# Three inner norms of a two-layer encoder, with the tokens run in two halves

## What is computed

```python
for layer in range(2):
    h = rms_norm(x, norm_mix_pre[layer])
    m = even_mixer(h, ...) if layer == 0 else odd_mixer(h, ...)   # both end in @ w_out, 1024 x 1024
    x = x + rms_norm(m, norm_mix_post[layer])
    h = rms_norm(x, norm_ffn_pre[layer])
    u = causal_dwconv(h @ w_up, conv_w, conv_b)      # w_up 1024 x 5632, three taps
    g, val = u[..., :2816], u[..., 2816:]
    f = (gelu(g) * val) @ w_down                     # 2816 x 1024
    x = x + rms_norm(f, norm_ffn_post[layer])
```

## Time and profile before

| what | value |
|---|---|
| three runs | 1189.26, 1192.99, 1192.96 us; median 1192.96 |
| the profiled execution | 1188.73 us; its span 1186.9 us |
| TensorE busy | 1149.5 us, 97% of the span |
| VectorE, ScalarE, GpSimd busy | 58%, 41%, 6% |
| mean granted TensorE clock | 0.993 of full speed |
| HBM read | 98.02 MB |
| load of a 1 MB unit | 5.1 us from issue to landing (median) |
| what ends the chain: TensorE, VectorE, ScalarE | 84%, 7%, 6% of the span |

### The profile page before, as it was taken

The page is one execution under the profiler, slowest core; times in us unless marked ns, Lnnn a source line. Parts: engine busy times, 40 slices in busy tenths (PEclk is TensorE's granted clock), DMA queues, the critical chain, the costliest instruction groups (busy, mean ns, idle before and its releaser), DMA issues.

```text
span 1186.9 us, 14989 instructions
## 1 busy us (share of the span) xinstructions
PE 1149.5 (97%) x5888; PEld 959.4 (81%) x5888; DVE 692.9 (58%) x840; ACT 486.1 (41%) x667; POOL 73.2 (6%) x57
## 2 busy tenths in 40 slices
PE   8999999999999999999999998899999999999997
PEld 6875777777888888888887788786888888899997
DVE  5745455558876766732228677248877766752222
ACT  4555655434533443431123229334444443433220
POOL 3000000122000000000112100033000000000000
PEclk9999999999999999999999999999999999999999
DMA  6312112222333332322321541041423333332221
GB/s 212 107 36 72 36 36 71 71 72 71 107 84 93 106 104 77 103 98 98 98 98 36 156 129 49 1 126 34 135 79 105 106 88 88 106 98 65 96 99 71
DMA packets 147477, 104.39 MB, mean 88 GB/s; under 512 B 4642, under 2 KB 144354, under 8 KB 147426
## 3 DMA queue, kind: packets, MB, share of 16 engines
q1 hardware_dynamic: 146466, 102.36, 29.0%
q10 hardware_dynamic: 960, 1.31, 0.5%
HBM read 98.02 MB, written 2.10 MB: 84 GB/s over the span
## 4 chain that ended last, share of the span: by engine, by line
PE 84%; DVE 7%; ACT 6%; issue 1%; POOL 0%; DMA 0%; POOLq 0%; SPq 0%; DVEq 0%; ACTq 0%
PE ps L1283 25%; PE ps L1285 25%; PE ps L1284 25%; DVE x L1076 3%; PE ps L1480 2%; PE ps L1468 2%; ACT hx_hi L656 1%; DVE hx_lo L1080 1%; ACT prob L772 1%; PE ps L1491 1%; PE ps L1352 1%; ACT w_hi L522 1%; PE ps L1345 1%; PE ps L1504 1%; PE ps L1660 1%
## 5 line engine op out<-in xcount | busy, mean ns | idle before, releaser
L1283 PE MATMUL ps<-hx_hi,w_hi 128*128 128x512 f32 x912 | 360.5, 395 | 2.7 <-DVE hx_lo L1080 2.5
L1284 PE MATMUL ps<-hx_lo,w_hi 128*128 128x512 f32 x912 | 355.9, 390 | 0.0
L1285 PE MATMUL ps<-hx_hi,w_lo 128*128 128x512 f32 x912 | 355.7, 390 | 0.0
L810 DVE TENSOR_TENSOR w_lo<-w_raw,w_hi 128x2048 fp32r<-128x2048 f32 (+1 forms) x90 | 201.9, 2243 | 169.5 <-ACT w_hi L522 169.4
L522 ACT ACTIVATE w_hi<-w_raw 128x2048 fp32r<-128x2048 f32 (+1 forms) x90 | 168.4, 1871 | 159.2 <-DMA w_raw<-in_ffn_w_down 113.8
L1283 PEld LDWEIGHTS ps<-hx_hi,w_hi 128*128 128x128 f32 x912 | 171.5, 188 | 45.8 <-DVE hx_lo L1080 7.2
L1285 PEld LDWEIGHTS ps<-hx_hi,w_lo 128*128 128x128 f32 x912 | 171.6, 188 | 36.3
L1284 PEld LDWEIGHTS ps<-hx_lo,w_hi 128*128 128x128 f32 x912 | 171.7, 188 | 35.2 <-issue 0.7
L1283 PE MATMUL ps<-w_hi,g_hi 128*128 128x256 f32 x352 | 99.2, 282 | 0.0
L1285 PE MATMUL ps<-w_hi,g_lo 128*128 128x256 f32 x352 | 98.9, 281 | 0.0
L1284 PE MATMUL ps<-w_lo,g_hi 128*128 128x256 f32 x352 | 98.9, 281 | 0.0
(11 more groups left out here) (202 smaller groups left out, 1524.1 us busy)
## 6 DMA issues: line engine op xcount, KB each, us to landing
w_raw<-in_ffn_w_up SPq DMA_DIRECT2D x88, 512.0 KB, 5.0
w_raw<-in_ffn_w_down SPq DMA_DIRECT2D x16, 1024.0 KB, 5.1
w_raw<-in_even_w_in SPq DMA_DIRECT2D x8, 1024.0 KB, 5.1
w_raw<-in_ffn_w_down SPq DMA_DIRECT2D x8, 768.0 KB, 4.4
w_raw<-in_odd_w_qkv SPq DMA_DIRECT2D x6, 1024.0 KB, 5.0
w_raw<-in_even_w_out SPq DMA_DIRECT2D x4, 1024.0 KB, 5.1
w_raw<-in_odd_w_o SPq DMA_DIRECT2D x4, 1024.0 KB, 5.7
x_in<-in_x SPq DMA_DIRECT2D x4, 512.0 KB, 6.4
```

Of the source, the lines that this page charges most:

```text
L810: dve.tensor_tensor(w_lo[s][:, 0:k], w_raw[s][:, 0:k], w_hi[s][:, 0:k], ALU.subtract).then_inc(w_lo_done, 1)
L1283: pe.matmul(dst, s_hi, r_hi, start=first, stop=False)
L1284: pe.matmul(dst, s_hi, r_lo, start=False, stop=False)
L1285: return pe.matmul(dst, s_lo, r_hi, start=False, stop=last)
```

## The change

Tokens 0 to 255 are half A, 256 to 511 half B. Around each inner norm, work that took all 512 tokens at once is done for A and then for B: the last three pieces of an output projection (the last piece of the down projection), the norm after it with the addition to x and the split into hx_hi and hx_lo, and the first two units of the next product. TensorE does A of the last pieces, then B of them, with the mean square and the spread of A put between B's k-steps (before steps 3 and 7); then A of the first unit, with B's mean square before its k-step 3; A of the second unit, with B's spread before k-step 1; then B of both units, tile by tile. Matmuls of these stretches have 256 columns where they had 512, and there are twice as many.

The pre-norm squares of whole tiles are made while half B is normed. Its mean square goes before k-step 6 of the first tile of the third unit and its spread before k-step 1 of that unit's second tile. Squares have three buffers; of the last square of each half no sum is made on GpSimd, TensorE takes it directly (6 products of one column for each half, where there were 8 for all tokens). The splits of the weights of the first three units of the next product lie inside the norm: unit 0's in half A after tile 2 (ScalarE) and tile 4 (VectorE), unit 1's between the halves, unit 2's in half B. The filler matmuls of keep_clock are gone at these three places. The early k-steps of piece 2 of the first output projection are done later, with the rest of that piece. The second output projection does piece 0 alone where it did pieces 0 and 1 together. In the sliding-window attention the eight small products of a chunk are issued in the order 0, 4, 1, 5, 2, 6, 3, 7.

```diff
+HALF = T // 2
+HALVED = {U_UP[0], U_UP[0] + 1, U_QKV, U_QKV + 1, U_UP[1], U_UP[1] + 1}
...
@@ GpSimd
+        def half_sums(bi, h):
+            for j in range(2):
+                q = 2 + 3 * h + j
+                pool.wait_ge(psq_done, post_squares(bi) + q + 1)
+                for b in range(2):
+                    pool.wait_ge(psum_done, post_sums(bi) + 1 + 4 * h + 2 * j + b)
+                    pool.tensor_tensor(sumsq[:, tokens_of(h)], sumsq[:, tokens_of(h)], sq[q % 3][:, tokens_of(b)], ALU.add).then_inc(psum_done, 1)
...
@@ ScalarE
+        def boundary(bi, which, layer, last, u):
+            def hi(h, i):
+                act.wait_ge(x_new, 2 * DT * bi + DT * h + i + 1)
+                act.activation(hx_hi[:, i, tokens_of(h)], x[:, i, tokens_of(h)], ACT.Identity,
+                               scale=gain(which, layer, i)).then_inc(hx_hi_done, 1)
+            act.preload_act_table_set("sqrt_and_others")
+            for j, v in enumerate(last):
+                half_square(bi, 0, j, v)
+            post_root(bi, 0)
+            if len(last) > 1:
+                half_square(bi, 1, 0, last[0])
+            for i in range(DT):
+                hi(0, i)
+                if i == 2:
+                    split_hi(u)
+                if i == 4 and len(last) > 1:
+                    half_square(bi, 1, 1, last[1])
+            half_square(bi, 1, len(last) - 1, last[-1])
+            split_hi(u + 1)
+            post_root(bi, 1)
+            for i in range(DT):
+                hi(1, i)
+                square(bi + 1, i, x[:, i, :])
+                if i == 4:
+                    split_hi(u + 2)
+            root(bi + 1)
...
@@ VectorE
+            def normed(h, i):
+                mi = m[:, i, tokens_of(h)]
+                dve.scalar_tensor_tensor(out=mi, in0=mi, scalar=gain(*post, i), in1=bank(6 + h)[:, 0:HALF],
                                          op0=ALU.mult, op1=ALU.mult).then_inc(post_t, 1)
+            for j, v in enumerate(last):
+                half_copy(bi, 0, j, v)
+            post_inverse(bi, 0)
+            if len(last) > 1:
+                half_copy(bi, 1, 0, last[0])
+            for h in range(2):
+                dve.wait_ge(pbc_mm, 2 * bi + h + 1)
+                normed(h, 0)
+                add(h, 0)
+                for i in range(DT):
+                    if i + 1 < DT:
+                        normed(h, i + 1)
+                    lo(h, i)
+                    if i + 1 < DT:
+                        add(h, i + 1)
+                    if h == 0 and i == 3 and len(last) > 1:
+                        half_copy(bi, 1, 1, last[1])
+                    if h == 0 and i == 4:
+                        split_lo(u)
+                    if h == 1 and i == 5:
+                        split_lo(u + 2)
+                if h == 0:
+                    half_copy(bi, 1, len(last) - 1, last[-1])
+                    post_inverse(bi, 1)
+                    split_lo(u + 1)
+            inverse_rms(bi + 1)
+            spread(bi + 1)
+            dve.wait_ge(rbc_done, bi + 2)
...
@@ TensorE
+        def post_mean_square(bi, h):
...
+            for t in (2 * h, 2 * h + 1):
+                c = P * (t - 2 * h)
+                srcs = (sumsq[:, P * t:P * t + P], sq[q % 3][:, c:c + P], sq[q % 3][:, HALF + c:HALF + c + P])
+                for i, src in enumerate(srcs):
+                    last = pe.matmul(bank(7)[:, t:t + 1], src, ones[:, 0:1], start=i == 0 and t == 2 * h, stop=i == 2 and t == 2 * h + 1)
+            last.then_inc(pms_mm, 1)
...
+        def first_half(u, h, k):
+            for b in range(2):
+                dst = bank(group_banks(group_of(u)) + h)[:, tokens_of(b)]
+                ins = three(dst, *weights(u, k, b), hx_hi[:, k, tokens_of(h)], hx_lo[:, k, tokens_of(h)], k == 0 and b == 0,
+                            k == UK - 1 and b == 1)
+            return ins
...
-        def boundary(n, bi, u):
-
-            mean_square(n)
-            keep_clock(7, 6)
-            spread(n)
-            keep_clock(13, 7)
-            first_two(u, lambda k: pe.wait_ge(hx_ready, DT * (bi + 1) + k + 1),
-                      fill=lambda k: mean_square(n + 1) if k == DT - 1 else None)
-            spread(n + 1)
+        def out_halves(layer):
+            bi = 2 * layer
+            ks = {1: rest if layer == 0 else range(UK), 2: range(UK), 3: range(UK)}
+            for h in range(2):
+                step = 0
+                for j in (1, 2, 3):
...
+                    for k in ks[j]:
+                        if h and step == 3:
...
+                            post_mean_square(bi, 0)
+                        if h and step == 7:
+                            post_spread(bi, 0)
+                        step += 1
+                        last = out_half(layer, j, h, k, k == 0 and (layer, j) != (0, 1), k == UK - 1)
+                    last.then_inc(unit_done if h else ahalf_mm, 1)
...
+        def first_units(bi, u):
...
+            for j in range(2):
+                unit_ready(u + j)
+                for k in range(UK):
+                    if j == 0 and k == 3:
+                        post_mean_square(bi, 1)
+                    if j == 1 and k == 1:
+                        post_spread(bi, 1)
+                    pe.wait_ge(hx_ready, DT + 2 * DT * bi + k + 1)
+                    first_half(u + j, 0, k)
+            pe.wait_ge(group_evac, evac)
+            for k in range(UK):
+                pe.wait_ge(hx_ready, 2 * DT + 2 * DT * bi + k + 1)
+                for j in range(2):
+                    last = first_half(u + j, 1, k)
+                    if k == UK - 1:
+                        last.then_inc(unit_done, 1)
+            unit(u + 2, hx, hooks={(0, 6): lambda: mean_square(bi + 1), (1, 1): lambda: spread(bi + 1)})
...
@@ TensorE, values of the sliding-window attention
-            for e in range(8):
+            for e in (0, 4, 1, 5, 2, 6, 3, 7):
```

More of the change, by code:

```diff
@@ L54 @@
 G_SHIFT = N_DOWN - 4
-def n_sums(n):
-    return DT - 1 if n % 2 == 0 else DT - 2
-def sums_before(n):
-    return sum(n_sums(i) for i in range(n))
+HALF = T // 2
+N_BOUNDARY = 3
 V_CONV = 64
@@ L515, in _ @@
+        half_sums(0, 1)
+        pre_norm(1)
+        whole_sums(1, 6)
+        pre_norm(2)
+        pool.wait_ge(rope_raw, 2)
+        for a in range(2):
+            pool.memset(kz[a][HD * (1 - a):HD * (1 - a) + HD], 0.0).then_inc(kz_zeroed, 1)
+        whole_sums(2, 2)
+        half_sums(2, 0)
+        half_sums(2, 1)
+        pre_norm(3)
     @block.scalar
@@ L1047, in _, with m_copy @@
         rotary_signs()
[L1049 removed]
+        def m_copy(bi, i, u):
             for b in range(2):
[L1051 to L1054 removed]
+                dve.wait_ge(psq_done, post_squares(bi) + 2 * i + b + 1)
+                ins = dve.tensor_copy(m[:, 2 * i + b, :], bank(group_banks(group_of(u)) + b))
@@ L1537, in _ @@
         pe.wait_ge(yb_ready, 6)
-        out_part(0, ready, first=True)
+        out_whole(0, ready, first=True)
         sb_cum(SB_HEADS - 1)
@@ new lines, in down_halves @@
+        def down_halves():
+            for h in range(2):
+                for c, (k0, k1) in enumerate(DOWN_K):
+                    u = U_DOWN[0] + 9 + c
+                    if h == 0:
+                        unit_ready(u)
+                        if c == 0:
+                            banks_free(group_of(u))
+                    for k in range(k0, k1):
+                        if h and k == 3:
+                            post_mean_square(1, 0)
+                        if h and k == 7:
+                            post_spread(1, 0)
+                        last = down_half(u, h, k, k0)
+                    if h:
+                        last.then_inc(unit_done, 1)
+                if h == 0:
+                    last.then_inc(ahalf_mm, 1)
@@ L1572, in ffn @@
+        def out_projection(layer):
+            if layer == 1:
+                pe.wait_ge(y_ready, NCH)
+                banks_free(group_of(U_OUT[1]))
+                unit_ready(U_OUT[1])
+                out_whole(1, range(UK), first=True, end=True)
+            out_halves(layer)
         def ffn(layer, bi):
             u0 = U_UP[layer]
-            n = 4 * layer + 1
-            boundary(n, bi, u0)
-            for j in range(2, 5):
+            first_units(bi, u0)
+            for j in range(3, 5):
@@ L1583, in ffn @@
             g_up = group_of(U_DOWN[layer])
-            for mp in range(4):
+            for mp in range(3 + layer):
                 b0 = group_banks(g_up + mp)
@@ L1618, in _ @@
         ffn(0, 0)
-        boundary(3, 1, U_QKV)
-        for k in range(2, N_QKV):
+        down_halves()
+        first_units(1, U_QKV)
+        for k in range(3, N_QKV):
             u = U_QKV + k
```

364 lines of the change are left out of this document (201 added, 163 removed).

## The result

| kernel | median | lowest to highest | runs |
|---|---|---|---|
| before | 1191.89 us | 1189.26 to 1192.99 | 4 |
| after | 1219.61 us | 1213.38 to 1223.15 | 4 |

The ratio is 1.0231, with a 95% interval of 1.0204 to 1.0258: the change costs some 27.5 us. The forecast was 1211, its range 1194 to 1220. Two things stand out before any row is read: the time is only 0.4 us inside the upper end of the range (two of the four executions, at 1223 us, lie outside it), and the four executions after lie 10 us apart, where those before lie within 4. The profiled execution after is the fastest of the four (1213.38 us, mean granted clock 0.981; the slowest had 0.974), so its own difference to the profiled one of before is 24.65 us.

A forecast was written before the change was run, and what follows sets the result against it. TensorE, 97% busy, was taken as the bound, with VectorE under 1 us of slack at the sixth unit. +6.8 + 5.8 + 7.9 - 0.8 = +19.7 gave 1208.4 (profiled) or 1212.7 (median), so 1211 us; range 1194 to 1220.

The forecast's parts named there:

- TensorE's start without early k-steps: First norm: TensorE waits for ya_lo to about 215.7; the count starts at 222.6, 2.8 us earlier, 18 matmuls still to do.
- The halves: Last three pieces, first norm: half A ends 15.1 us and half B 31.8 us after the count's start.
- Half A's chain: Half A's norm: a tile takes 1.39 us; the first unit's w_lo is complete at 35.1 us, the eighth tile at 38.7.
- Waits before the first unit: TensorE waits 3.4 us for the first unit's w_lo, then 1.3 us at B's mean square for the last square.
- Half B and the lock: Half B's norm: VectorE's two-SBUF-operand operations and GpSimd's sums wait for each other (the lock), 5 us more; TensorE waits 4.7.
- The late scale: Behind the norm: rbc starts 8.1 us after the third unit, before 0.6; sixth unit at 104.6 where it would be 103.3.
- last-slack reading: Trace of the kernel before: VectorE catches up only with the sixth up unit, less than 1 us of slack there.
- Attention: Small products: alternating column halves may give 0 to -3.4 us; -0.8 us was taken.
- Net per norm: Loss at each inner norm: +6.8 us in the first, +5.8 in the middle, +7.9 in the third.
- a rival of 20%: The clock falls behind TensorE's new waits in each norm: 3 to 9 us more in all, 1214 to 1220; chance 20%.
- The rival that halves hide the norm: All waits between piece 0 and the third unit gone, 9.4 to 10 us per norm: 1181 to 1185; chance 12%.

The follow-up runs named there:

- run 9: Run 7's kernel with ScalarE's and VectorE's splits for the first unit two tiles earlier in half A: 1208.49 us, ratio 1.0145 to the kernel before.
- run 4: The changed kernel with filler matmuls of 256 columns, whose result nothing reads, where TensorE waits: 1210.17 us, ratio 1.0167 to the kernel before.
- Run 3: The changed kernel with GpSimd's pre-norm sums two to seven cut from 512 columns to 8 (not a usable kernel): 1201.35 us, ratio 1.0104.
- run 8: The kernel before with GpSimd's pre-norm sums two to seven cut from 512 columns to 8 (not a usable kernel): 1175.54 us, ratio 0.9884.
- run 1: The kernel before with the pre-norm's mean square and spread issued late, inside the third unit: 1203.55 us, ratio 1.0118.
- run 2: The changed kernel with the pre-norm's mean square and spread issued at the start of the third unit: 1204.02 us, ratio 1.0119 to the kernel before.
- run 5: The kernel before with only the attention's eight small products reordered to 0, 4, 1, 5, 2, 6, 3, 7: 1189.90 us, ratio 0.9994.
- run 10: Run 7's kernel with 22 filler matmuls before the first unit's half A and 12 before half B's seventh tile: 1192.48 us, ratio 1.0012.
- run 6: The kernel before with GpSimd's pre-norm sum i waiting until VectorE's add of tile i + 2 is done: 1176.03 us, ratio 0.9880.
- run 7: Run 2's kernel with GpSimd's pre-norm sum i waiting for the add of half B's tile i + 2: 1193.82 us, ratio 1.0028.

## Why the prediction was right, and where it was short

The sign, the places and most of the sizes held; the sum of 19.7 us was 24.65 in the profiled execution, and the medians are 27.5 apart. The steps below count from where piece 0 (in the middle norm piece 2) is done, in the changed kernel at 221.7, 603.9 and 781.8 us:

1. **TensorE's start without early k-steps**: it waited for ya_lo until 214.76; the forecast said 215.7, and the count starts 0.9 us before its 222.6.
2. **The halves**: half B ended at 253.88 (256.94 - 3.06), 32.1 behind the count's start; forecast 31.8.
3. **Half A's chain**: first w_lo complete at 256.84, so 35.1 behind the start, as forecast. A tile takes 1.40 us, 1.39 was forecast.
4. **Waits before the first unit**: 3.06 us, forecast 3.4; run 9 took it off by an earlier split and lost more elsewhere.
5. **Half B and the lock**: third unit 67.3, 67.2 and 70.4 us behind the count's start in the three norms, forecast 65.9, 66.0 and 70.0. TensorE waits 3.34 us there and not 4.7, but its last two tiles behind the wait take 4.47 us (284.53 to 289.00), where run 4, with the clock at 1.00, has 2.98 (287.01 to 289.99). hx_lo does wait (1.12 for 0.48), as was taken without a row. Run 3 gives the lock 5 us per norm. What the forecast did not say is that before the change the lock cost nearly as much (run 8): it explains next to none of the slowdown.
6. **The late scale**: rbc 75.4, 75.3 and 78.5, forecast 74.0, 74.1 and 78.1. Its worth was shown from both sides: 14 us put in (run 1), 13 taken out (run 2, the clock's part with it), half of the whole. The last-slack reading of the earlier trace rows, under 1 us before the sixth unit, was what mattered.
7. **Attention**: -0.8 was forecast, +1.0 read; the shorter rows are real and worth nothing that run 5 could show (at most 2 us).
8. **Net per norm**: +7.8, +6.9 and +8.9 in place of +6.8, +5.8 and +7.9. Each is 1 us more.

**The step that fell short** is the choice to leave the clock out of the sum and keep it as a rival of 20%. It said that "each norm may have 2 to 6 us at the lower level, part of them under waits anyhow: 3 to 9 us more in all". There were 10.2, 13.6 and 10.2 us in the three norms, nine stretches in all. The reading of the earlier trace rows had the stretch of the kernel before as two microseconds long; it went on to 3.4. Run 4 gives the price in all, some 7.5 us by the ratios, which lies in the rival's 3 to 9. With the fillers the halved kernel is 19.9 us behind the kernel before (0.0167 x 1190), and the forecast without the clock was 19.7. That agreement is in part luck: run 4 keeps two of the nine stretches, the interval of each ratio is some 2 to 3 us to either side, and between the two profiled executions the fillers gave 3.1 us and not 7.5. Luck too is that the median lies in the range at all, by 0.4 us. Forecast and this rival were no alternatives: the one brings the waits that the other needs, and their chances should have been added into one case at 1214 to 1220. The rival that halves hide the norm had against it what it was said to have, and no run came near it: even with the late scale, the lock and the waits' clock seen to (run 10) the halved kernel isn't faster than before.

What stays open: the 17 to 18 us between run 6 and runs 7 and 10 were not split by a run. The rows of run 7 show three candidates. TensorE's waits of 0.4 us and more inside the half stretches are 6.2 us in the first norm (3.06, 1.20 and 1.98: w_lo, the last square, the seventh tile), 3.9 in the middle one and 5.2 in the third. Its clock is at half rate for 13.6 us in the norms, in run 6 for 3.4. And the halves themselves cost, by an estimate from the forecast's spacings (0.2354 us for a pair, 0.227 for the whole; 222, 228 and 240 pairs in the three norms), up to 5.8 us. How the 17 to 18 us divide among them is not shown.

## What to carry to other kernels

Cutting work into halves to hide a norm can help only if the in-order engines beside TensorE have room, and here they had too little: each half brought a wait of its own, and the scale moved to a later place on a chain that had under 1 us of slack. Before restructuring, look for a row that is longer than its twins: the add of 1.77 us beside 0.69 was the cheapest gain found in this kernel: one wait that reverses who comes first, GpSimd's sum or VectorE's add, 1.2% for two lines. Price each new wait of TensorE with the stretch of lower clock that it may bring behind it (here mostly 3.4 us at half rate, at times 6.8 or 10.2), and place a split no earlier than its load can have landed.

## What the runs showed of the hardware that was not expected

- The fall of the granted clock behind a wait is not the same from one execution to the next: behind waits of 3.25 and 3.23 us of the same stage it was 3.4 and 10.2 us at 1.2 GHz, behind one of 1.96 some 3.4 (0.24 x 7 / 0.5), and behind one of 3.06 the clock held for 5 us, until after another wait of 1.20. The changed kernel, with nine such waits, spread over 10 us in four executions, and over 0.9 with fillers under them.
- An operation that meets a running sum pays at most for the rest of it. For VectorE's operations of two SBUF operands of 512 columns that was 1.08 us with the sum issued 0.1 us ahead and 0.43 us with it issued 0.66 us ahead, while normed, with one operand in PSUM, ran in 0.74 us under the sum.
- Eight small products issued so that neighbours write alternate halves of the output's partitions took 1.09 us a chunk in place of 1.58 (the forecast had left open whether anything would change). It held in the changed kernel and, as the only edit, in run 5.
